# ScalarE's squares of the second token block's first half, moved between two groups of the first block's hand-over

## The chip, the core and the metric

The kernel runs on one core of a Trainium2 chip. The metric is the device time of one execution in microseconds (us), median of three runs.

## What is computed

Two transformer blocks over one sequence of 256 tokens with 1024 features, each with two layers, all in fp32:

```python
# first block, per layer
h = modulate(x, norm_g[l, 0], sh1, sc1)          # rms_norm(x) * g * (1 + scale) + shift
x = x + 0.5 * g1 * swiglu(h, w_ffn1_gu[l], w_ffn1_down[l])
h = modulate(x, norm_g[l, 1], sh2, sc2)
x = x + g2 * (three kinds of attention(h @ w_in[l]) @ w_out[l])
h = modulate(x, norm_g[l, 2], sh3, sc3)
x = x + 0.5 * g3 * swiglu(h, w_ffn2_gu[l], w_ffn2_down[l])
# second block, per layer
h = modulate_2(rmsnorm(x, norm1[l]), sh1, sc1)
x = x + g1 * (retention and pooling branches(h @ w_in[l]) @ w_out[l])
h2 = modulate_2(rmsnorm(x, norm2[l]), sh2, sc2)
x = x + g2 * ((silu(gate) * up) @ w_ffn_out[l])
```

rms_norm divides each token's row by the root of the mean of its squares plus eps. This root needs the squares of all 1024 features of a token.

## The kernel before

The 256 tokens are two token blocks t = 0 and 1 of 128 partitions each (`x[:, t, :]`). The work is ten phases (six in the first block, four in the second), each a list of products of the split activations with streamed weights. An fp32 product is made of three matmuls: `products` (L1911 to L1913) multiplies the high part of the activations with the high and the low part of the weights, and the low part with the high. Weights come by DMA from the SP queue into `weights_raw`. ScalarE rounds a unit of 128x1024 to its high part (`hi_static`, L750), VectorE subtracts to get the low part (`lo_static`, L1221), and TensorE may start a unit when the semaphore `lo_done` has counted it. The order of instructions on every engine is written out by hand; each engine works through its own queue in that order.

Between two phases lies a **hand-over**. There are nine (phase k = 2 to 10 begins with one), and the kernel's end has code of its own. In a hand-over these things happen:

- VectorE (`boundary`) multiplies the four accumulators, two token blocks by two halves of 512 columns, by the gate (L1366) and adds three of them to x (L1372). The add of block 1, first half, is GpSimd's (L732), which then counts `x_late`.
- ScalarE (`norm_stage`) takes the squares of x with their row sums (`squares`, L770; the first half also adds eps, L772), the square root (`root`, L776), waits for VectorE's reciprocal (`x_stats`, L1312), and scales x into `xn` (`scale_x`, L782). For block 1 VectorE scales the first 512 columns in two pieces (`x_scale1`, L1318, semaphore `xn1a_ready`), and ScalarE the last 512 (`xn1b_ready`).
- TensorE turns `xn` (transposes, `x_turn`, L2027) in pairs of 128 columns. With t and the pair that makes eight **groups**: groups 0 to 3 are block 0, groups 4 to 7 block 1.
- Each group is scaled and shifted by the modulation (`x_scaled`: groups 2, 3, 4 and 6 on ScalarE, L791; 0, 1, 5 and 7 on VectorE, L1327), rounded by ScalarE (`x_hi`, L798), and its low part is taken by VectorE (`x_low`, L1336, semaphore `hlo_done`).
- TensorE (`first_strip`) multiplies group by group. In block 0 each group u also uses a new weight unit. The group's first chunk ends with the transposes of block 1's first two pairs only in group 3:

```python
                    if t == 0:
                        pe.wait_ge(S("lo_done"), n + u + 1)
                    pe.wait_ge(S("hlo_done"), tr[0] + g + 1)
                    for c in range(2):
                        if k > 1 and t == 0 and u == 3 and c == 1:
                            x_turn(1, (0, 1), k)
```

Three of the four weight units have their low halves before the hand-over or at its start. The fourth's stands in VectorE's queue right behind the low parts of groups 2 and 3:

```python
                    x_low(2)
                    x_low(3)
                    lo_static(end + PREFETCH - 1, SLOT)
                x_stats(k + 1, 1)
                x_scale1(k + 1)
```

`then` puts a wait behind an instruction: the next one of the same engine starts only when the step has been counted. `squares` uses it after the squares and after the eps.

Of the kernel before, what the change touches and what calls it, by code (L numbers as in the profile page):

```python
# [238 lines left out]
def need(eng, sem, value):  # L239

    if not isinstance(value, int) or value > 0:
        eng.wait_ge(sem, value)


def build(nc, A, out):
    with ExitStack() as ctx:
# [5 lines left out]
        def S(name):  # L252
            if name not in sems:
                sems[name] = ctx.enter_context(nc.semaphore(name))
            return sems[name]
# [170 lines left out]
        def x_group(g, i):  # L426

            t, j = divmod(X_FIRST[g] if i == 0 else g, 4)
            return hf[:, (i + g) % 4, :].rearrange("p (k n) -> p k n", k=2), (slice(2 * j, 2 * j + 2), slice(P * t, P * (t + 1)))

        def x_chunk(g, i, k, first):

            b, c0 = X_AT_FIRST[X_FIRST[g]] if first else X_AT[g]
            return hf[:, (i + g) % 4, P * k:P * (k + 1)], bank[b][:, c0 + P * k:c0 + P * (k + 1)]

        def x_is_scaled(eng, k, g):

            on_act = X_BY_ACT_FIRST if k == 1 else X_BY_ACT
            by = [i for i in range(X_GROUPS) if (i in on_act) == (g in on_act)]
            eng.wait_ge(S("scaled_by_act" if g in on_act else "scaled_by_dve"), len(by) * (k - 1) + by.index(g) + 1)  # L440
# [295 lines left out]
        def _(act):  # L736
            seq = [0]

            def then(ins):

                seq[0] += 1
                ins.then_inc(S("act_step"), 1)
                act.wait_ge(S("act_step"), seq[0])
# [16 lines left out]
            def squares(k, t, h):  # L760

                if k == 1:
                    act.wait_ge(S("x_loaded"), 16)
                elif (t, h) == (1, 0):
                    act.wait_ge(S("x_late"), k - 1)
                else:
                    act.wait_ge(S("x_done"), 3 * (k - 2) + (1, 2, 0, 3)[2 * t + h])
                c = slice(512 * h, 512 * (h + 1))
                at = stat[:, 2 * t + h:2 * t + h + 1]
                then(nc.scalar.activation(xn[:, t, c], x[:, t, c], ACT.Square, scale=D ** -0.5, accum_out=at))  # L770
                if h == 0:
                    then(nc.scalar.activation(at, at, ACT.Identity, bias=stat[:, S_EPS:S_EPS + 1]))  # L772

            def root(k, t):

                nc.scalar.activation(stat[:, 4 + t:5 + t], stat[:, 2 * t + 1:2 * t + 2], ACT.Sqrt, bias=stat[:, 2 * t:2 * t + 1])\  # L776
                    .then_inc(S("rms_ready"), 1)
                act.wait_ge(S("rstd_ready"), 2 * (k - 1) + t + 1)

            def scale_x(t, c0, c1, sem):  # L780

                nc.scalar.activation(xn[:, t, c0:c1], x[:, t, c0:c1], ACT.Copy, scale=stat[:, 6 + t:7 + t]).then_inc(S(sem), 1)  # L782

            def x_scaled(a, g, first=False):

                act.wait_ge(S("tr_ready"), turned[0] + (4 + X_FIRST[g] // 4 * 4 if first else X_TURNED[g]))
                need(act, S("hlo_done"), tr[0] + g - 3)
                for k in range(2):
                    c = 2 * ((X_FIRST[g] if first else g) % 4) + k
                    to, src = x_chunk(g, tr[0], k, first)  # L790
                    ins = nc.scalar.activation(to, src, ACT.Identity, scale=sclA[:, c:c + 1], bias=modc[:, 8 * a["mod"] + c:8 * a["mod"] + c + 1])  # L791
                ins.then_inc(S("scaled_by_act"), 1)

            def x_hi(g):

                src, at = x_group(g, tr[0])
                x_is_scaled(act, o_n[0], g)
                nc.scalar.activation(hhi[:, at[0], at[1]], src, ACT.Copy).then_inc(S("hhi_done"), 1)  # L798
# [5 lines left out]
            def norm_stage(k, after):  # L804

                squares(k, 0, 0)
                squares(k, 0, 1)
                root(k, 0)
                for c0, c1 in ((0, 256), (256, 512), (512, 1024)):
                    scale_x(0, c0, c1, "xn0_ready")  # L810
                if after is not None:
                    split_block0(after)
                squares(k, 1, 0)
                squares(k, 1, 1)
                root(k, 1)
                scale_x(1, 512, 1024, "xn1b_ready")
                if after is not None:
                    split_block1(after)

            def split_block0(after):  # L820

                act.wait_ge(S("scale_ready"), o_n[0])
                x_hi(0)
                x_scaled(after[2], 2)
                x_hi(1)
                x_hi(2)
                x_scaled(after[2], 3)
                x_hi(3)

            def split_block1(after):  # L830

                x_scaled(after[2], 4)
                x_hi(4)
                x_hi(5)
                x_scaled(after[2], 6)
                x_hi(6)
                x_hi(7)
                x_split_done()
# [43 lines left out]
            def first_phase(a):  # L882
# [19 lines left out]
                x_hi(7)  # L902
                x_split_done()
            norm_stage(1, None)

            for kind, n0, a in phases:
                o_n[0] += 1
                if o_n[0] > 1:
                    norm_stage(o_n[0], (kind, n0, a))
                else:  # L910
                    first_phase(a)
# [44 lines left out]
                elif kind == "mid1":  # L956
# [110 lines left out]
                    for h in range(12):  # L1067
                        k = 12 * m + h
# [1496 lines left out]
```

## Time and profile before

| | |
|---|---|
| runs | 1797.13, 1795.12, 1795.99 us; median 1795.99 us |
| the profiled execution's own time | 1796.07 us |
| its span | 1794.2 us |
| granted TensorE clock, mean | 0.997 |
| TensorE matmul busy | 1756.8 us, 98% of the span |
| VectorE busy | 1334.3 us, 74% |
| ScalarE busy | 925.9 us, 52% |
| GpSimd busy | 183.3 us, 10% |

The span runs from the first to the last recorded work; 1.87 us of the execution's own time lie around it. In the trace PE is TensorE (PEld its weight loads), ACT is ScalarE, DVE is VectorE, POOL is GpSimd. Matmuls are pipelined, so that one of 0.39 us starts 0.23 us after the one before it.

### The profile page before, as it was taken

To read this page: it belongs to the slowest core of one execution; us is meant where nothing else is said; L and a number is where in the kernel's file an instruction comes from. 1 tells how busy PE (TensorE), PEld (TensorE's weight loads), DVE (VectorE), ACT (ScalarE), POOL (GpSimd) and SP (SyncE) were. 2 spreads that over 40 slices of the span, in tenths; PEclk is the share of its full clock that TensorE was granted. 3 is DMA by queue.
4 is the path that set the end of the run, shared out by engine and by line. 5 is a ranking of instruction groups with operands and counts; after the bars stand their busy time and mean duration, and the time that the engine had idled before them with its cause. 6 is when DMAs were issued, how large, how long until landed. Compare 5 with 4: busy or idle time off the path is not lost.

```text
span 1794.2 us, 23576 instructions
## 1 busy us (share of the span) xinstructions
PE 1756.8 (98%) x8820; PEld 1449.3 (81%) x8820; DVE 1334.3 (74%) x1977; ACT 925.9 (52%) x1509; POOL 183.3 (10%) x382
## 2 busy tenths in 40 slices
PE   6999999999999999999999999999999999999998
PEld 3778888788878888887888788888888788878886
DVE  6988977778788777768787866478787775677455
ACT  4444577744364345767444644456334644464434
POOL 3111012111111111021110000001110000010000
PEclk9999999999999999999999999999999999999999
DMA  9999832699859885517898664559897484566561
GB/s 328 362 345 368 298 129 75 235 337 336 308 205 353 316 322 204 161 65 270 307 354 291 205 206 156 186 170 329 312 328 262 153 295 156 178 214 237 192 210 72
DMA packets 241874, 441.03 MB, mean 246 GB/s; under 512 B 15248, under 2 KB 157408, under 8 KB 241632
## 3 DMA queue, kind: packets, MB, share of 16 engines
q1 hardware_dynamic: 207760, 315.98, 51.8%
q0 software_dynamic: 33296, 120.12, 17.4%
q10 hardware_dynamic: 704, 3.42, 0.5%
q8 instruction: 70, 1.15, 0.3%
q14 instruction: 44, 0.36, 0.1%
HBM read 438.38 MB, written 1.09 MB: 245 GB/s over the span
## 4 chain that ended last, share of the span: by engine, by line
PE 89%; DVE 5%; ACT 3%; DMA 2%; issue 1%; SPq 0%; DVEq 0%; ACTq 0%
PE bank L1911 27%; PE bank L1913 27%; PE bank L1912 27%; PE bank L2087 2%; DVE weights_lo L1221 1%; DMA weights_raw<-in_w_mod_first 1%; DMA weights_raw<-in_w_ffn_gu 1%; DVE x L1372 1%; DVE arena L1366 1%; PE bank L2277 1%; PE bank L2305 1%; ACT arena L791 0%; ACT hT_hi L798 0%; PE bank L2027 0%; PE bank L2276 0%
## 5 line engine op out<-in xcount | busy, mean ns | idle before, releaser
L1221 DVE TENSOR_TENSOR weights_lo<-weights_raw,weights_hi 128x1024 fp32r<-128x1024 f32 (+2 forms) x584 | 673.1, 1200 | 130.7 <-ACT weights_hi L750 129.6
L1911 PE MATMUL bank<-weights_hi,hT_hi 128*128 128x512 f32 (+2 forms) x1696 | 670.2, 395 | 8.7 <-DVE hT_lo L1336 8.7
L1913 PE MATMUL bank<-weights_hi,hT_lo 128*128 128x512 f32 (+2 forms) x1696 | 658.4, 388 | 0.0
L1912 PE MATMUL bank<-weights_lo,hT_hi 128*128 128x512 f32 (+2 forms) x1696 | 657.2, 388 | 0.0
L750 ACT ACTIVATE weights_hi<-weights_raw 128x1024 fp32r<-128x1024 f32 (+2 forms) x584 | 569.0, 1038 | 103.6 <-PE bank L1913 33.0
L1911 PEld LDWEIGHTS bank<-weights_hi,hT_hi 128*128 128x128 f32 x1696 | 318.6, 188 | 75.6 <-DVE hT_lo L1336 6.7
L1913 PEld LDWEIGHTS bank<-weights_hi,hT_lo 128*128 128x128 f32 x1696 | 318.3, 188 | 65.4
L1912 PEld LDWEIGHTS bank<-weights_lo,hT_hi 128*128 128x128 f32 x1696 | 318.9, 188 | 59.5
L1234 DVE CUSTOM_DVE_ANT_0 arena<-arena,mod_acc,vectors 128x1024 f32<-128x1024 f32 x216 | 264.3, 1279 | 0.0
L926 ACT ACTIVATE actT_hi<-bank 128x512 fp32r<-128x512 f32 x66 | 39.6, 599 | 433.2 <-PE bank L2087 433.2
L1911 PE MATMUL bank<-weights_hi,actT_hi 128*128 128x512 f32 (+1 forms) x616 | 240.1, 390 | 1.9 <-DVE weights_lo L1221 1.4
L1913 PE MATMUL bank<-weights_hi,actT_lo 128*128 128x512 f32 (+1 forms) x616 | 237.9, 386 | 0.0
L1912 PE MATMUL bank<-weights_lo,actT_hi 128*128 128x512 f32 (+1 forms) x616 | 237.8, 386 | 0.0
L1515 DVE TENSOR_TENSOR actT_lo<-bank,actT_hi 128x512 fp32r<-128x512 f32 x66 | 45.6, 690 | 133.2 <-ACT actT_hi L926 133.2
L1911 PEld LDWEIGHTS bank<-weights_hi,actT_hi 128*128 128x128 f32 x616 | 115.6, 188 | 27.9 <-DVE actT_lo L1515 2.8
L1913 PEld LDWEIGHTS bank<-weights_hi,actT_lo 128*128 128x128 f32 x616 | 115.6, 188 | 23.3
L1912 PEld LDWEIGHTS bank<-weights_lo,actT_hi 128*128 128x128 f32 x616 | 115.7, 188 | 22.3
L477 POOL DMA_DIRECT2D arena<-in_w_mod x128 | 67.9, 532 | 362.3 <-DVE mod_cols L1234 359.1
L732 POOL TENSOR_TENSOR x<-x,arena 128x512 f32<-128x512 f32 x10 | 13.2, 1324 | 703.7 <-DVE arena L1366 703.7
L921 ACT ACTIVATE arena<-bank 128x256 f32<-128x256 f32 x132 | 43.6, 383 | 70.3 <-PE bank L1913 70.3
L477 POOL DMA_DIRECT2D arena<-in_w_ada x88 | 46.8, 534 | 258.4 <-DVE mod_cols L1234 251.8
L1510 DVE TENSOR_TENSOR arena<-arena,bank 128x256 f32<-128x256 f32 x132 | 49.2, 414 | 18.9 <-ACT arena L921 18.9
(282 smaller groups left out, 1179.0 us busy)
## 6 DMA issues: line engine op xcount, KB each, us to landing
weights_raw<-in_w_ffn_gu SPq DMA_DIRECT2D x176, 512.0 KB, 5.7
arena<-in_w_mod POOLq DMA_DIRECT2D x128, 512.0 KB, 6.9
weights_raw<-in_w_in SPq DMA_DIRECT2D x104, 512.0 KB, 4.7
weights_raw<-in_w_ffn_down SPq DMA_DIRECT2D x88, 512.0 KB, 5.2
arena<-in_w_ada POOLq DMA_DIRECT2D x88, 512.0 KB, 6.8
weights_raw<-in_w_ffn_in SPq DMA_DIRECT2D x88, 512.0 KB, 5.4
weights_raw<-in_w_ffn_out SPq DMA_DIRECT2D x44, 512.0 KB, 4.5
weights_raw<-in_w_out SPq DMA_DIRECT2D x32, 512.0 KB, 4.2
```

The lines of the kernel that those rows point to most:

```text
L477: eng.dma_start(mod_tile(m), mod_rows(m)).then_inc(S(mod_sem(m)), 16)
L750: nc.scalar.activation(whi[:, n % PARTS, 0:width], raw[:, slot, 0:width], ACT.Copy).then_inc(S("hi_done"), credit(n))
L921: nc.scalar.activation(sg_t[:, t, :], bank[gu_banks(j)[t]][:, 0:256], ACT.Silu).then_inc(S("silu_done"), 1)
L926: nc.scalar.activation(ahi[:, j % 2].rearrange("p k n -> p (k n)"), bank[ATB][:, :], ACT.Copy)\
L1221: V.tensor_tensor(wlo[:, n % PARTS, 0:width], raw[:, n % RING, 0:width], whi[:, n % PARTS, 0:width].bitcast(F32), ALU.subtract).then_inc(S ...
L1234: V.tensor_tensor_reduce(modw[m % MOD_RING], modw[m % MOD_RING], cond_row, 1.0, vec[:, m:m + 1], ALU.mult, ALU.add, modc[:, m:m + 1])\
L1510: ins = V.tensor_tensor(act_t[:, t, :], sg_t[:, t, :], bank[gu_banks(j)[t]][:, 256:512], ALU.mult)
L1515: V.tensor_tensor(alo[:, j % 2].rearrange("p k n -> p (k n)"), bank[ATB][:, :], ahi[:, j % 2].rearrange("p k n -> p (k n)").bitcast(F32), ...
L1911: T.matmul(o, sh, wh, start=start, stop=False)
L1912: T.matmul(o, sh, wl, start=False, stop=False)
L1913: return T.matmul(o, sl, wh, start=False, stop=stop)
L2087: ins = T.transpose(bank[ATB][:, 256 * k + P * t:256 * k + P * (t + 1)], act_t[:, t, P * k:P * (k + 1)], ident)
```

## The change

In each of the nine hand-overs ScalarE's squares of block 1, first half (`squares(k, 1, 0)`: square with row sum, then eps) are issued behind the rounding of group 2 and ahead of the scaling of group 3. They stood behind the rounding of group 3. Phase 1, which has no such split (`after is None`), keeps its order. Nothing is added or left out.

```diff
                 if after is not None:
-                    split_block0(after)
-                squares(k, 1, 0)
+                    split_block0(k, after)
+                if after is None:
+                    squares(k, 1, 0)
                 squares(k, 1, 1)
                 root(k, 1)
                 scale_x(1, 512, 1024, "xn1b_ready")
...
-            def split_block0(after):
+            def split_block0(k, after):
 
                 act.wait_ge(S("scale_ready"), o_n[0])
                 x_hi(0)
                 x_scaled(after[2], 2)
                 x_hi(1)
                 x_hi(2)
+                squares(k, 1, 0)
                 x_scaled(after[2], 3)
                 x_hi(3)
```

ScalarE's queue in the first hand-over, before. `hT_hi` is the rounded group, `arena<-bank4` the scaling of groups 2 and 3, `arena,stat<-x` the squares with row sum, `stat<-stat` first the eps, then the root:

```order
L791 ACTIVATE arena<-bank4,mod_cols,scale_cols 128x128 [waits hlo_done,tr_ready]
L791 ACTIVATE arena<-bank4,mod_cols,scale_cols 128x128
L798 ACTIVATE hT_hi<-arena 128x2x128 [waits scaled_by_dve]
L798 ACTIVATE hT_hi<-arena 128x2x128 [waits scaled_by_act]
L791 ACTIVATE arena<-bank4,mod_cols,scale_cols 128x128 [waits hlo_done,tr_ready]
L791 ACTIVATE arena<-bank4,mod_cols,scale_cols 128x128
L798 ACTIVATE hT_hi<-arena 128x2x128 [waits scaled_by_act]
L770 ACTIVATE arena,stat<-x 128x512 [waits x_late]
L772 ACTIVATE stat<-stat 128x1 [waits act_step]
L770 ACTIVATE arena,stat<-x 128x512 [waits x_done,act_step]
L776 ACTIVATE stat<-stat 128x1 [waits act_step]
L782 ACTIVATE arena<-x,stat 128x512 [waits rstd_ready]
```

The same place in the changed kernel:

```order
L791 ACTIVATE arena<-bank4,mod_cols,scale_cols 128x128 [waits hlo_done,tr_ready]
L791 ACTIVATE arena<-bank4,mod_cols,scale_cols 128x128
L798 ACTIVATE hT_hi<-arena 128x2x128 [waits scaled_by_dve]
L798 ACTIVATE hT_hi<-arena 128x2x128 [waits scaled_by_act]
L770 ACTIVATE arena,stat<-x 128x512 [waits x_late]
L772 ACTIVATE stat<-stat 128x1 [waits act_step]
L791 ACTIVATE arena<-bank4,mod_cols,scale_cols 128x128 [waits hlo_done,tr_ready,act_step]
L791 ACTIVATE arena<-bank4,mod_cols,scale_cols 128x128
L798 ACTIVATE hT_hi<-arena 128x2x128 [waits scaled_by_act]
L770 ACTIVATE arena,stat<-x 128x512 [waits x_done]
L776 ACTIVATE stat<-stat 128x1 [waits act_step]
L782 ACTIVATE arena<-x,stat 128x512 [waits rstd_ready]
```

The pair L770, L772 has moved ahead of group 3's three instructions; the wait on `act_step` behind the eps now stands on the scaling of group 3, no longer on the second squares.

VectorE's queue in the same hand-over is not reordered. It stands so in both kernels (line numbers of before): the low parts of groups 2 and 3, the fourth unit's low half, the reciprocal of block 1, and its first columns scaled:

```order
L1372 TENSOR_TENSOR x<-x,arena 128x512 [waits x_gated]
L1336 TENSOR_TENSOR hT_lo<-arena,hT_hi 128x2x128 [waits hhi_done,scaled_by_act] x2
L1221 TENSOR_TENSOR weights_lo<-weights_raw,weights_hi 128x1024 [waits hi_done]
L1312 RECIPROCAL stat<-stat 128x1 [waits rms_ready]
L1318 TENSOR_SCALAR arena<-x,stat 128x256 [waits rstd_ready]
```

What the second of the two low parts waits for (`hhi_done`) is the rounding of group 3 that the change sets later.

## Rows read from the trace of the kernel before

**Rows 1.** The page, chain of waits that ended last, by engine.

```profile
PE 89%; DVE 5%; ACT 3%; DMA 2%; issue 1%; SPq 0%; DVEq 0%; ACTq 0%
```

**Rows 2.** TensorE's waits: us in total, times, longest.

```profile
PE bank L1911 <- DVE hT_lo L1336: 8.7, 19, 2.5
```

**Rows 3.** Timeline of TensorE, seventh hand-over: start, us, instruction, idle before it.

```profile
1211.60 0.47 PE L1911 MATMUL bank<-weights_hi,hT_hi 128*128 128x512 f32 x1 [0.18 <-DVE hT_lo L1336]
...
1215.86 0.39 PE L1911 MATMUL bank<-weights_hi,hT_hi 128*128 128x512 f32 x1
...
1216.54 0.60 PE L2027 MATMUL bank<-con,arena 128*128 128x128 f32 x4
...
1216.90 0.48 PE L1911 MATMUL bank<-weights_hi,hT_hi 128*128 128x512 f32 x1
...
1218.80 0.50 PE L1911 MATMUL bank<-weights_hi,hT_hi 128*128 128x512 f32 x1 [0.52 <-DVE hT_lo L1336]
...
1219.13 0.39 PE L1912 MATMUL bank<-weights_lo,hT_hi 128*128 128x512 f32 x1
```

**Rows 4.** Timeline of ScalarE, seventh hand-over.

```profile
1211.91 0.72 ACT L798 ACTIVATE hT_hi<-arena 128x256 fp32r<-128x256 f32 x2
1212.52 0.80 ACT L791 ACTIVATE arena<-bank,mod_cols,scale_cols 128x128 f32<-128x128 f32 x2
1213.36 0.42 ACT L798 ACTIVATE hT_hi<-arena 128x256 fp32r<-128x256 f32 x1
1213.68 0.62 ACT L770 ACTIVATE arena<-x 128x512 f32<-128x512 f32 x1
1214.20 0.19 ACT L770 ACTIVATION_READ_ACCUMULATOR arena<-x 128x1 f32 x1
1214.42 0.29 ACT L772 ACTIVATE stat<-stat 128x1 f32<-128x1 f32 x1
1214.75 0.63 ACT L770 ACTIVATE arena<-x 128x512 f32<-128x512 f32 x1
...
1215.51 0.29 ACT L776 ACTIVATE stat<-stat 128x1 f32<-128x1 f32 x1
```

**Rows 5.** Timeline of VectorE, seventh hand-over.

```profile
1211.03 0.42 DVE L1336 TENSOR_TENSOR hT_lo<-arena,hT_hi 128x256 fp32r<-128x256 f32 x1 [0.30 <-ACT hT_hi L798]
...
1213.37 0.93 DVE L1336 TENSOR_TENSOR hT_lo<-arena,hT_hi 128x256 fp32r<-128x256 f32 x2
1214.22 1.22 DVE L1221 TENSOR_TENSOR weights_lo<-weights_raw,weights_hi 128x1024 fp32r<-128x1024 f32 x1
1215.83 0.16 DVE L1312 RECIPROCAL stat<-stat 128x1 f32<-128x1 f32 x1 [0.39 <-ACT stat L776]
1216.03 0.62 DVE L1318 TENSOR_SCALAR arena<-x,stat 128x256 f32<-128x256 f32 x2
...
1218.32 0.42 DVE L1336 TENSOR_TENSOR hT_lo<-arena,hT_hi 128x256 fp32r<-128x256 f32 x1 [0.41 <-ACT hT_hi L798]
```

**Rows 6.** Timeline of GpSimd, seventh hand-over.

```profile
1209.29 1.27 POOL L732 TENSOR_TENSOR x<-x,arena 128x512 f32<-128x512 f32 x1 [174.78 <-DVE arena L1366]
```

**Rows 7.** Timeline of VectorE, fourth and fifth hand-over: the fourth unit's low half.

```profile
718.44 1.21 DVE L1221 TENSOR_TENSOR weights_lo<-weights_raw,weights_hi 128x1024 fp32r<-128x1024 f32 x1
...
827.67 1.22 DVE L1221 TENSOR_TENSOR weights_lo<-weights_raw,weights_hi 128x1024 fp32r<-128x1024 f32 x1
```

**Rows 8.** Timeline of TensorE, fourth and fifth hand-over: first matmul of group 3.

```profile
720.18 0.39 PE L1911 MATMUL bank<-weights_hi,hT_hi 128*128 128x512 f32 x1
...
829.24 0.39 PE L1911 MATMUL bank<-weights_hi,hT_hi 128*128 128x512 f32 x1
```

**Rows 9.** Stretches early in phase 1: busy time (count) of each engine, then PEclk.

```profile
22.00:24.00 2.00, 1.78 (x52) 0.95 (x53) 1.21 (x4) 0.76 (x3) 0.00 (x0) 0.53 1.01 406
24.00:26.00 2.00, 2.00 (x16) 1.37 (x14) 1.90 (x7) 1.54 (x2) 0.00 (x0) 0.61 1.07 422
...
34.00:36.00 2.00, 0.71 (x6) 0.50 (x5) 1.96 (x6) 1.06 (x4) 0.00 (x0) 1.00 0.87 309
```

## The prediction

> **What bounds the kernel now.** I read the chain of waits first: 89% of it is TensorE's own work [rows 1]. So a change can pay, or cost, only where TensorE stands still. TensorE's list of waits is next: its largest wait beyond the very start is for the low part of the activations (L1336), 8.7 us in 19 times, the longest 2.5 us [rows 2]. That longest one is in phase 1. The other 18 are two in each of the nine hand-overs: 0.18 us before group 0 and about half a microsecond before group 4 (0.18 and 0.52 us in the seventh [rows 3]). The timelines of the nine hand-overs are alike to a tenth of a microsecond, so I work in the seventh and scale up.
>
> The order of events there is what a reader should see. TensorE starts group 3 at 1215.86, turns block 1's first pairs at 1216.54, goes on at 1216.90, and stands before group 4, which starts at 1218.80 [rows 3]. ScalarE has **no gap** where the change works: rounding of groups 1 and 2 (1211.91, two), scaling of 3 at 1212.52, rounding of 3 at 1213.36, squares at 1213.68, eps at 1214.42, second squares at 1214.75, root at 1215.51 [rows 4]. None of these rows carries an idle time. VectorE takes the low parts of groups 2 and 3 from 1213.37 to 1214.30, then the low half of the fourth weight unit from 1214.22 to 1215.44, then waits 0.39 us for ScalarE's root and takes the reciprocal at 1215.83 [rows 5].
>
> **The moved block.** It is two instructions, squares with row sum and eps. From its start to the start of the next squares it takes 1214.75 - 1213.68 = 1.07 us of ScalarE [rows 4]. The Trainium skill would have it shorter: its page "ScalarE: Activation LUTs", section "What ACT_TABLE_LOAD costs", gives 186 ns + 0.833 ns a column for an ACTIVATE with immediates, 93 ns more for a pointer operand, and 93 ns of overlap between neighbours, which I make an estimate of 613 + 280 - 93 = 800 ns. The rows show why that is not the block here: the read of the row sum (0.19 us at 1214.20) and the wait for it lie between the two [rows 4]. By the page's 0.80 the sum below would be 9 x (0.80 + 0.06 + 0.10) - 3.74 = 4.90 us, by the row it is 7.33; I take the row.
>
> **What becomes earlier: nothing that counts.** Squares and eps move to about 1212.5, where the scaling of group 3 stands now, but the second squares cannot start earlier: the engine has the same instructions ahead of them, with no gap to fill. The wait on the eps moves from the second squares to the scaling of group 3, and is as long there (eps ends at 1214.71, next start 1214.75 [rows 4]). So root 1 stays at 1215.51. Its own wait for GpSimd's addition costs nothing: that ends at 1209.29 + 1.27 = 1210.56, two microseconds before the squares' new place [rows 4, 6]. No DMA is issued by the block, and no table load stands at either place.
>
> **What becomes later.** Scaling and rounding of group 3, by 1.07 us. The rounding ends at 1213.36 + 0.42 = 1213.78; the low part of group 3 starts at 1214.30 - 0.42 = 1213.88, 0.10 us behind it [rows 4, 5]. So VectorE already follows ScalarE here, and goes back with it in full: the fourth unit's low half starts at 1214.22 + 1.07 = 1215.29 and ends at 1216.51. **TensorE needs this unit for group 3** (its wait on lo_done), which it now starts at 1215.86. Before, the low half was ready at 1215.44, 0.42 us early; now it is late. The slack is the start of group 3 less the end of the low half. Over the nine hand-overs it is 0.50, 0.37, 0.42, 0.53, 0.35, 0.38, 0.42, 0.38 and 0.39 us, together 3.74; the largest is the fourth (720.18 - 719.65), the smallest the fifth (829.24 - 828.89) [rows 7, 8].
>
> Behind the end of a VectorE instruction TensorE needs a moment. Group 4 starts 0.06 us after the low part's end (1218.32 + 0.42 = 1218.74 to 1218.80), group 0 needs 0.15 (1211.45 to 1211.60) [rows 3, 5]. Group 3's wait, with matmuls running right up to it, is nearer to the first in kind (only the instruction just before differs), so 0.06; 0.15 is kept as the high end. A stopped stream also starts slowly: after the wait the second matmul comes 0.33 us behind the first (1218.80, 1219.13), where three in flow take 1216.54 - 1215.86 = 0.68, 0.23 each [rows 3]. That is 0.10 us more; the low end is none.
>
> In the seventh: 1.07 - 0.42 + 0.06 + 0.10 = **0.81 us**. In all nine: 9 x (1.07 + 0.06 + 0.10) - 3.74 = **7.33 us**.
>
> **Is it given back?** After group 3's first chunk come the transposes of block 1, and all up to group 4 hangs on them: 1218.80 - 1216.54 = 2.26 us [rows 3]. They would be at 1217.35. What they need is VectorE's scaled columns. The reciprocal now stands behind the late low half: at about 1216.43 instead of 1215.83, 0.60 us later, so the two pieces end at 1216.65 + 0.60 = 1217.25 [rows 5], just in time. ScalarE's part of the scaling follows the same reciprocal and is back by 1217.35, ahead of the scaling of group 4. So the wait before group 4 keeps its half microsecond, and behind it TensorE works without a stop up to the next hand-over, so that there is no gap in which it could catch up. At most the transposes lose the few hundredths that some hand-overs now wait for the second piece. The last hand-over, at the kernel's end, is untouched.
>
> **The sum.** 1796.07 (the profiled execution) + 7.33 = 1803.40; that execution is 0.08 us above the median, so 1803.3. The bounds: without the slow start and the 0.06, 9 x 1.07 - 3.74 = 5.89, which is 1801.9; with 0.15 for the semaphore, 8.14, which is 1804.1. Runs of this kernel lie about 1 us to either side of their median.
>
> **Rivals.** *No change:* the late low half is covered after all, because TensorE does not stand at group 3 when it comes. For it: the shift is only 0.65 us beyond the slack. Against it: TensorE's timeline has group 3 directly behind group 2 in all nine, with no gap. It decides if the shift is under 0.42 us. Time: 1796.0. *Faster:* the squares fill a gap of ScalarE, root and reciprocal come up to 1.07 us earlier, and the wait before group 4 goes. That wait is (8.7 - 2.5 - 9 x 0.18) = 4.6 us in all [rows 2, 3], so 1791.4. It would need ScalarE to stand idle between the rounding of group 2 and the scaling of group 3 for longer than the slack it spends; the rows show no idle there at all, and the transposes could not start before group 3's first chunk ends anyway [rows 3, 4]. *The clock falls:* TensorE would stand still for 0.7 us more, and soon after for 0.5. Early in phase 1 the granted clock was 0.53 and 0.61 in two stretches of 2 us, between the levels of 1.2 and 2.4 GHz, after a stretch of small matmuls with gaps; in 34 to 36 us TensorE stood still for most of the time and the clock stayed at 1.00 [rows 9]. Such a dip would cost 2 x 0.47 + 2 x 0.39 = 1.7 us, nine of them 15.5 us: 1818.8. The Trainium skill ("TensorE: Matmul & The Clock Gate", "What's actually happening") has the throttled state as the default that activity lifts. By that rule more idle time speaks for this rival; the stretch at full clock beside the wait of 2.5 us [rows 2, 9] speaks against it.
>
> **Chances.** Forecast 0.87; no change 0.07; faster 0.03; clock 0.03. A difference of 0.2%, 3.6 us, is about what a measurement of this kernel can tell from none. The forecast and the clock case are slower by more than that: 0.90. No change is 0.07, faster 0.03. The range is the forecast's own, since it alone holds 8 in 10: from 1801.9 and 1804.1, widened by the spread of runs of 1.1 us at both ends: 1800.7 to 1805.3.
>
> **What would show it.** In the changed profile: a new wait of TensorE ahead of group 3 (line 1911, now 1913) for the weights' low half (line 1221, now 1223), nine times, 0.6 to 0.8 us each. The squares directly behind the rounding of group 2; VectorE idle about 1 us before the second low part and none before the reciprocal; the wait before group 4 still about 0.5 us; the root at the same distance from group 0. Wrong would be: group 3 directly behind group 2; the root earlier; the wait before group 4 gone or doubled; granted clock below 1 in a hand-over.

## The result and the profile after

| | before | changed |
|---|---|---|
| median of six runs each | 1796.22 us (1794.81 to 1797.15) | 1802.54 us (1802.15 to 1804.65) |
| ratio, with its 95% interval | | 1.0036 [1.0026, 1.0047] |
| the profiled execution's own time | 1796.07 us | 1802.21 us |
| its span | 1794.2 us | 1800.4 us |
| VectorE, ScalarE busy | 1334.3, 925.9 us | 1334.0, 925.5 us |
| granted TensorE clock, mean | 0.997 | 0.997 |

The change makes the kernel slower by 0.36%, 6.3 us. A second set of six runs (below) gave 1802.93 against 1795.76, 7.2 us. The forecast was 1803.3 us, with a range of 1800.7 to 1805.3.

TensorE's waits in the changed kernel (us in total, times, longest) are to be held against [rows 2]. The lines of the kernel have moved by two:

```profile
PE bank L1913 <- DVE hT_lo L1338: 8.9, 19, 2.5
PE bank L1913 <- DVE weights_lo L1223: 6.5, 10, 1.3
```

The kernel before has this row in place of the second:

```profile
PE bank L1911 <- DVE weights_lo L1221: 1.4, 1, 1.4
```

The first row is what it was, 8.7 before and 8.9 now. In the second, TensorE now waits for a low half of weights ten times. One of these, the longest, is in phase 1 and was there before. The other nine are new, one in each hand-over, ahead of group 3, of 0.47, 0.61, 0.59, 0.56, 0.59, 0.58, 0.60, 0.56 and 0.59 us, together 5.15.

TensorE in the seventh hand-over (start, us, instruction, idle before it), to be held against [rows 3]. Group 0 started at 1215.29:

```profile
1219.26 0.39 PE L1915 MATMUL bank<-weights_hi,hT_lo 128*128 128x512 f32 x1
1220.25 0.50 PE L1913 MATMUL bank<-weights_hi,hT_hi 128*128 128x512 f32 x1 [0.60 <-DVE weights_lo L1223]
1220.58 0.39 PE L1914 MATMUL bank<-weights_lo,hT_hi 128*128 128x512 f32 x1
...
1221.04 0.60 PE L2029 MATMUL bank<-con,arena 128*128 128x128 f32 x4
...
1223.30 0.50 PE L1913 MATMUL bank<-weights_hi,hT_hi 128*128 128x512 f32 x1 [0.53 <-DVE hT_lo L1338]
```

Group 3 starts at 1220.25 after a wait of 0.60 us for the weights' low half; the next matmul comes 0.33 us behind it. From the transposes at 1221.04 on everything keeps its old distances: group 4 comes 2.26 us later, after the same half microsecond of waiting.

ScalarE at the same place, to be held against [rows 4]:

```profile
1215.58 0.72 ACT L798 ACTIVATE hT_hi<-arena 128x256 fp32r<-128x256 f32 x2
1216.20 0.63 ACT L770 ACTIVATE arena<-x 128x512 f32<-128x512 f32 x1
1216.72 0.20 ACT L770 ACTIVATION_READ_ACCUMULATOR arena<-x 128x1 f32 x1
1216.95 0.29 ACT L772 ACTIVATE stat<-stat 128x1 f32<-128x1 f32 x1
1217.28 0.81 ACT L791 ACTIVATE arena<-bank,mod_cols,scale_cols 128x128 f32<-128x128 f32 x2
1218.12 0.42 ACT L798 ACTIVATE hT_hi<-arena 128x256 fp32r<-128x256 f32 x1
1218.44 0.62 ACT L770 ACTIVATE arena<-x 128x512 f32<-128x512 f32 x1
...
1219.18 0.29 ACT L776 ACTIVATE stat<-stat 128x1 f32<-128x1 f32 x1
1220.30 0.73 ACT L782 ACTIVATE arena<-x,stat 128x512 f32<-128x512 f32 x1 [0.83 <-DVE stat L1314]
```

The squares and the eps stand between the rounding of group 2 and the scaling of group 3, and take 1217.28 - 1216.20 = 1.08 us. The root is at 1219.18. Behind it ScalarE waits 0.83 us for the reciprocal; in the kernel before it waits 0.23 us there. VectorE, against [rows 5]:

```profile
1218.64 0.43 DVE L1338 TENSOR_TENSOR hT_lo<-arena,hT_hi 128x256 fp32r<-128x256 f32 x1 [1.17 <-ACT hT_hi L798]
1218.98 1.22 DVE L1223 TENSOR_TENSOR weights_lo<-weights_raw,weights_hi 128x1024 fp32r<-128x1024 f32 x1
1220.11 0.15 DVE L1314 RECIPROCAL stat<-stat 128x1 f32<-128x1 f32 x1
1220.30 0.67 DVE L1320 TENSOR_SCALAR arena<-x,stat 128x256 f32<-128x256 f32 x2
```

It waits 1.17 us for the rounding of group 3, takes its low part, then the fourth unit's low half, and comes to the reciprocal with no wait of its own. Counted from the start of group 0, in us (the forecast worked out from the prediction's numbers):

| seventh hand-over | before | forecast | changed |
|---|---|---|---|
| rounding of group 3 ends | 2.18 | 3.25 | 3.25 |
| fourth unit's low half starts | 2.62 | 3.69 | 3.69 |
| root of block 1 | 3.91 | 3.91 | 3.89 |
| reciprocal of block 1 | 4.23 | 4.83 | 4.82 |
| group 3 starts | 4.26 | 4.97 | 4.96 |
| transposes of block 1 | 4.94 | 5.75 | 5.75 |
| group 4 starts | 7.20 | 8.01 | 8.01 |

### The profile page after: what moved, and what is told of

It is laid out like the page before. It is cut to its first block, busy times and chain, and to the rows that moved or that the text cites. A ratio compares the mean times of both kernels' runs of the same rounds, so it can differ in the third digit from the quotient of the medians.

```text
span 1800.4 us, 23567 instructions
## 1 busy us (share of the span) xinstructions
PE 1759.2 (98%) x8820; PEld 1448.7 (80%) x8820; DVE 1334.0 (74%) x1977; ACT 925.5 (51%) x1509; POOL 184.9 (10%) x382
## 3 DMA queue, kind: packets, MB, share of 16 engines
HBM read 438.38 MB, written 1.09 MB: 244 GB/s over the span
## 4 chain that ended last, share of the span: by engine, by line
PE 87%; DVE 5%; ACT 4%; DMA 2%; issue 1%; SPq 0%; DVEq 0%; ACTq 0%
PE bank L1913 26%; PE bank L1915 26%; PE bank L1914 26%; DVE weights_lo L1223 2%; PE bank L2089 2%; ACT arena L791 1%; PE bank L2029 1%; DMA weights_raw<-in_w_mod_first 1%; ACT hT_hi L798 1%; DMA weights_raw<-in_w_ffn_down 1%; DVE x L1374 1%; DVE arena L1368 1%; ACT arena L770 1%; PE bank L2279 1%; PE bank L2307 1%
```

## The experiments

**The low half ahead of group 3's low part, in the changed kernel and in the one before.** If the fourth unit's low half is what TensorE waits for, it has only to stand ahead of the late group in VectorE's queue. The same swap in the kernel before is the control.

```diff
                     x_low(2)
-                    x_low(3)
                     lo_static(end + PREFETCH - 1, SLOT)
+                    x_low(3)
```

> The changed kernel, with the fourth unit's low half put ahead of the low part of group 3 in VectorE's queue. Theory (TensorE waits for that low half, which only stands behind the late group 3): it is ready at about 1.07 us less of a delay, the low part of group 3 ends about 0.4 us before TensorE comes to group 3, so the nine waits ahead of group 3 go, group 0 to group 4 takes 7.20 us as in the kernel before (8.02 in the changed one), and the time is that of before, 1796.2, within 1 us. Rival (the moved squares cost by themselves, through ScalarE or through the late group 3): the wait stays under another name and the time stays near 1802.5.

> The kernel before, with the same swap on VectorE and ScalarE's queue untouched. Theory (both were ready 0.35 us or more early): no change, 1796.2 within 1 us, no wait ahead of group 3. Rival (the swap is a gain or a loss of its own, so that the run above says nothing of the change): over 2 us off 1796.2.

Measured: the changed kernel with the swap 1796.74 us against 1795.93, ratio 1.0004 [0.9995, 1.0013]; the kernel before with it 1795.90, ratio 1.0005 [0.9996, 1.0014]. Neither differs from the kernel before by more than the runs can tell. VectorE in the changed kernel with the swap, seventh hand-over:

```profile
1214.89 1.22 DVE L1223 TENSOR_TENSOR weights_lo<-weights_raw,weights_hi 128x1024 fp32r<-128x1024 f32 x1
1216.15 0.43 DVE L1338 TENSOR_TENSOR hT_lo<-arena,hT_hi 128x256 fp32r<-128x256 f32 x1
1217.02 0.16 DVE L1314 RECIPROCAL stat<-stat 128x1 f32<-128x1 f32 x1 [0.44 <-ACT stat L776]
```

and TensorE (group 0 at 1212.77):

```profile
1217.03 0.39 PE L1913 MATMUL bank<-weights_hi,hT_hi 128*128 128x512 f32 x1
...
1219.97 0.50 PE L1913 MATMUL bank<-weights_hi,hT_hi 128*128 128x512 f32 x1 [0.52 <-DVE hT_lo L1338]
```

The low half ends at 1216.11, 0.92 us ahead of group 3's start at 1217.03. The low part of group 3, as late as in the changed kernel, still ends 0.45 us ahead. Group 4 starts 7.20 us after group 0, as before the change. Over all nine hand-overs the stretches from group 0 to group 4 are 64.80 us in this run and 64.84 in the control, against 64.85 in the kernel before and 72.22 in the changed one. The moved squares and the late group 3 themselves cost nothing: the loss is the one item queued behind them.

**Without the squares.** The rival "faster" rests on the root: would an earlier root remove the wait ahead of group 4?

```diff
-                squares(k, 1, 0)
+                if after is None:
+                    squares(k, 1, 0)
+                else:
+                    act.wait_ge(S("x_late"), k - 1)
                 squares(k, 1, 1)
```

> The kernel before without the squares of block 1, first half, in the nine hand-overs (left out: that half's part in the root; its wait for GpSimd's addition stays). ScalarE's root comes 1.07 us earlier. Theory (the transposes of block 1 are held by their place in TensorE's queue, behind group 3's first chunk, not by the root): the wait of half a microsecond ahead of group 4 stays and the time is 1795.8 to 1796.2, at most 0.05 us a hand-over better. Rival (the root sets the wait ahead of group 4): the wait goes, 1791.6.

Measured: 1795.23 us against 1795.93, ratio 0.9997 [0.9988, 1.0006]. That is 0.6 us below the range that was expected, but no difference that the runs can tell, and nowhere near the rival's 1791.6. Group 0 of the seventh hand-over started at 1211.64. ScalarE (root, scaling of x, scaling of group 4) and TensorE (transposes, group 4):

```profile
1214.46 0.29 ACT L776 ACTIVATE stat<-stat 128x1 f32<-128x1 f32 x1
1215.58 0.73 ACT L782 ACTIVATE arena<-x,stat 128x512 f32<-128x512 f32 x1 [0.83 <-DVE stat L1315]
1216.96 0.81 ACT L791 ACTIVATE arena<-bank,mod_cols,scale_cols 128x128 f32<-128x128 f32 x2 [0.65 <-PE bank L2030]
```

```profile
1216.54 0.60 PE L2030 MATMUL bank<-con,arena 128*128 128x128 f32 x4
...
1218.80 0.50 PE L1914 MATMUL bank<-weights_hi,hT_hi 128*128 128x512 f32 x1 [0.54 <-DVE hT_lo L1339]
```

The root now starts 2.82 us after group 0, 1.09 earlier than the 3.91 of before, and ScalarE stands idle behind it twice, for 0.83 and 0.65 us (0.23 and 0.21 before). The transposes come 4.90 us after group 0 (4.94 before), and group 4 still waits 0.54 us. Groups 0 to 4 take 64.78 us over the nine, 0.07 less than before. The root has slack, so no move of the squares alone could have gained anything.

**Less of the moved work.** If the cost is what the moved block exceeds the slack by, a shorter block must cost less. The eps stays in its old place, so the block is shorter by the pitch of one instruction (the argument True leaves the eps out of `squares`).

```diff
                 if after is None:
                     squares(k, 1, 0)
+                else:
+                    then(nc.scalar.activation(stat[:, 2:3], stat[:, 2:3], ACT.Identity, bias=stat[:, S_EPS:S_EPS + 1]))
...
-                squares(k, 1, 0)
+                squares(k, 1, 0, True)
                 x_scaled(after[2], 3)
```

> The changed kernel with the eps (L772) left in its old place, behind the rounding of group 3; only the square with its row sum stands ahead of the scaling of group 3. Theory (the cost is what the moved block exceeds the slack of the fourth unit's low half by): the block is 0.74 us instead of 1.07, so TensorE's waits ahead of group 3 shrink by 0.33 us each to 0.15 to 0.3 us, group 0 to group 4 takes 7.68 us in the seventh hand-over, and the time is 9 x (0.74 + 0.16) - 3.74 = 4.4 us over before, 1800.4. Rival (a broken stream costs a fixed amount, however late the unit is): as the changed kernel, 1802.5.

Measured: 1802.04 us (1799.55 to 1806.5) against 1796.27, ratio 1.0034 [1.0021, 1.0046]. By the median alone the rival would have it, but these six runs spread over 7 us. The hand-overs decide. TensorE in the seventh, groups 0, 3 and 4:

```profile
1216.97 0.47 PE L1915 MATMUL bank<-weights_hi,hT_hi 128*128 128x512 f32 x1 [0.18 <-DVE hT_lo L1340]
...
1221.62 0.50 PE L1915 MATMUL bank<-weights_hi,hT_hi 128*128 128x512 f32 x1 [0.28 <-DVE weights_lo L1225]
...
1224.68 0.50 PE L1915 MATMUL bank<-weights_hi,hT_hi 128*128 128x512 f32 x1 [0.52 <-DVE hT_lo L1340]
```

The wait ahead of group 3 is 0.28 us, where the changed kernel has 0.60, and group 4 comes 7.71 us after group 0, against 7.68 expected and 8.01 in the changed kernel. Over the nine, groups 0 to 4 take 4.6 us more than before (4.4 expected). The profiled execution took 1803.02 us; the rest of its time over the kernel before lies ahead of the first hand-over, which it reaches at 231.36 us, where the kernel before does so at 228.99. So the cost does follow the size of the block, as the hand-overs show; six runs that spread over 7 us cannot show it.

**A block shorter than the slack.** One short instruction of eps' kind stands in the squares' new place; the squares are left out so that the root can't interfere.

```diff
                 x_hi(2)
+                then(nc.scalar.activation(table_col[:, :], ones_col, ACT.Identity, bias=stat[:, S_EPS:S_EPS + 1]))
                 x_scaled(after[2], 3)
```

> The kernel of the run without the squares of block 1, first half (left out again), with one instruction of eps' length and a wait on it (on a scratch column, about 0.33 us) between the rounding of group 2 and the scaling of group 3. Theory (a block shorter than the slack of 0.35 to 0.53 us costs nothing): no wait ahead of group 3 above 0.05 us, group 0 to group 4 7.2 us, 1795.2 to 1796.2. Rival (every delay of group 3 is paid from its first nanosecond): 9 x 0.33 = 3.0 us, 1798.9.

Measured: 1796.77 us against 1796.27, ratio 1.0003 [0.9994, 1.0012]: 0.6 us above the range that was expected, but not the 3.0 us of the rival. VectorE (low part of group 3, low half) and TensorE (group 3 and group 4; group 0 at 1212.20), seventh hand-over:

```profile
1214.80 0.42 DVE L1340 TENSOR_TENSOR hT_lo<-arena,hT_hi 128x256 fp32r<-128x256 f32 x1 [0.41 <-ACT hT_hi L798]
1215.14 1.22 DVE L1225 TENSOR_TENSOR weights_lo<-weights_raw,weights_hi 128x1024 fp32r<-128x1024 f32 x1
```

```profile
1216.42 0.49 PE L1915 MATMUL bank<-weights_hi,hT_hi 128*128 128x512 f32 x1
1216.75 0.40 PE L1916 MATMUL bank<-weights_lo,hT_hi 128*128 128x512 f32 x1
...
1219.47 0.50 PE L1915 MATMUL bank<-weights_hi,hT_hi 128*128 128x512 f32 x1 [0.53 <-DVE hT_lo L1340]
```

No wait is listed ahead of group 3. But the low half ends at 1216.36, group 3 starts 0.06 us behind it, and its second matmul follows after 0.33 us, not 0.23. Groups 0 to 4 take 7.27 us. The nine hand-overs differ. In seven the low half ends 0.05 to 0.08 us ahead of group 3, and the second matmul comes after 0.31 to 0.34 us. In the first and the fourth it ends 0.22 and 0.21 us ahead, the second matmul comes after 0.23 us, and nothing is lost. Over the nine groups 0 to 4 take 0.76 us more than before, so the expectation of 7.2 was missed by a little: a unit that comes just in time costs a tenth of a microsecond though no wait shows.

**Statistics ahead of group 3.** If TensorE's order of transposes is what keeps the root from paying, both must move together. The root of block 1 goes ahead of group 3 on ScalarE, what depends on it goes ahead on VectorE, and on TensorE the transposes of block 1's first two pairs go ahead of group 3 and so fill the time in which it is not ready. (`sqrt_only` is `root` without its wait for the reciprocal, which now stands behind the rounding of group 3. The cut is against the changed kernel, and its definition is left out.)

```diff
                 if after is None:
                     squares(k, 1, 0)
-                squares(k, 1, 1)
-                root(k, 1)
+                    squares(k, 1, 1)
+                    root(k, 1)
...
                 squares(k, 1, 0)
+                squares(k, 1, 1)
+                sqrt_only(k, 1)
                 x_scaled(after[2], 3)
                 x_hi(3)
+                act.wait_ge(S("rstd_ready"), 2 * (k - 1) + 2)
...
                     x_low(2)
-                    x_low(3)
                     lo_static(end + PREFETCH - 1, SLOT)
                 x_stats(k + 1, 1)
                 x_scale1(k + 1)
                 if after is not None:
+                    x_low(3)
...
+                    if k > 1 and t == 0 and u == 3:
+                        x_turn(1, (0, 1), k)
                     if t == 0:
                         pe.wait_ge(S("lo_done"), n + u + 1)
                     pe.wait_ge(S("hlo_done"), tr[0] + g + 1)
                     for c in range(2):
-                        if k > 1 and t == 0 and u == 3 and c == 1:
-                            x_turn(1, (0, 1), k)
```

> Both halves' squares of block 1 and the root ahead of the scaling of group 3 on ScalarE; on VectorE the fourth unit's low half, the reciprocal and the two scaled pieces ahead of the low part of group 3; on TensorE the transposes of block 1's first two pairs ahead of group 3's first chunk, not behind it. Theory: group 3 is ready about 0.6 us late, but 0.36 us of that are filled by the transposes, and group 4's parts are ready as soon as TensorE comes to them: group 0 to group 4 takes about 6.7 us instead of 7.20, 1791.7 in all. Rival (the wait only moves ahead of group 3, whose rounding now stands behind 2.1 us of statistics): 7.2 to 7.6 us and 1796 to 1800.

Measured: 1792.47 us against 1795.93, ratio 0.9983 [0.9975, 0.9992]. It beats both kernels, if by 0.8 us less than expected. TensorE in the seventh hand-over (group 0, transposes, group 3, transposes, group 4):

```profile
1209.77 0.47 PE L1920 MATMUL bank<-weights_hi,hT_hi 128*128 128x512 f32 x1 [0.20 <-DVE hT_lo L1345]
...
1213.97 0.60 PE L2036 MATMUL bank<-con,arena 128*128 128x128 f32 x4
1214.63 0.47 PE L1920 MATMUL bank<-weights_hi,hT_hi 128*128 128x512 f32 x1
...
1216.08 0.60 PE L2036 MATMUL bank<-con,arena 128*128 128x128 f32 x4
1216.44 0.47 PE L1920 MATMUL bank<-weights_hi,hT_hi 128*128 128x512 f32 x1
1216.75 0.39 PE L1921 MATMUL bank<-weights_lo,hT_hi 128*128 128x512 f32 x1
```

Group 4 starts 6.67 us after group 0, and it does not wait any more (6.7 expected; 7.20 before). Over the nine hand-overs groups 0 to 4 take 60.24 us, 4.6 less than before. Yet from group 0 of the first hand-over to the end the profile is only 3.2 us shorter (table below), and the median 3.5. Most of the difference is given back in the two attention phases of the first block. Two rows of TensorE's list of waits:

```profile
PE bank L2138 <- DVE arena L1586: 1.2, 2, 0.6
PE bank L2036 <- ACT arena L786: 0.7, 1, 0.7
```

The first is 0.59 us in each of the two phases, where it was 0.19 and 0.14 before (L2129): 0.9 us given back. The second is the wait for ScalarE's scaled x at the end of the first of these phases. It scatters: 0.67 us here, 0.20 when this kernel was run again (below), 0.09 in the kernel before. In the other phases the stretch up to the next hand-over is 0.01 to 0.07 us longer each.

The trace shows where the first wait comes from. TensorE starts group 4 of the first hand-over 0.48 us earlier than before (6.80 us after group 0 against 7.28), but the last step of VectorE that it waits for has hardly moved. That step before, with group 0 at 228.99, and then in this run, with group 0 at 228.84:

```profile
247.30 0.28 DVE L1577 TENSOR_SCALAR arena<-arena,stat 128x128 f32<-128x128 f32 x1
```

```profile
247.11 0.28 DVE L1586 TENSOR_SCALAR arena<-arena,stat 128x128 f32<-128x128 f32 x1
```

It ends 18.59 us after group 0 before and 18.55 here. Ahead of it on VectorE stand the low halves of four weight units, which follow their rounding on ScalarE, and ScalarE's last rounding in that hand-over ends 8.46 us after group 0 before and 8.43 here. This is read from the trace; no run isolates it. Nor does this run, which moves work on three engines at once, show what each of the moves is worth by itself.

**Both once more, on one chip.** The changed kernel's median was 6.3 us above the kernel before, though its hand-overs were 7.4 us longer.

> The changed kernel once more, on the chip of the next run. The nine hand-overs' distances from group 0 to group 4 were 7.37 us longer in all in its profile, its median only 6.3 us longer over six runs, and the stretch ahead of the first hand-over, whose instructions are the same, was 1.0 us shorter. Theory (that stretch scatters from run to run, the hand-overs do not): from group 0 of the first hand-over to the end it is again 7.2 us longer than in the kernel before, within 0.3, and the median difference comes out at 7 us, within 1.5. Rival (about 1 us of the loss is given back ahead of the first hand-over): that stretch is again about 1 us shorter, and the median difference stays at 6.3 or below.

> The kernel with block 1's statistics ahead of group 3 once more. Theory: from group 0 of the first hand-over to the end 3.2 us shorter than in the kernel before, within 0.5, and a median 3.2 us shorter, within 1.5: nine times 0.53 us, less what two waits in the attention phases give back (about 0.5 us each) and a scattered wait. Rival (it gains nothing beyond scatter): within 1 us of the kernel before.

Measured: the changed kernel 1802.93 us against 1795.76, ratio 1.0044 [1.0031, 1.0057]; with the statistics ahead 1792.36, ratio 0.9981 [0.9972, 0.9989]. The profiled executions, split at group 0 of the first hand-over:

| kernel | ahead of it | from there to the end |
|---|---|---|
| before | 228.99 | 1567.08 |
| changed | 227.97 | 1574.24 |
| changed, once more | 228.90 | 1574.44 |
| changed, low half first | 229.83 | 1567.39 |
| before, low half first | 228.25 | 1567.33 |
| without the squares | 229.10 | 1566.91 |
| square alone moved | 231.36 | 1571.66 |
| short block | 229.20 | 1567.74 |
| statistics ahead of group 3 | 228.84 | 1563.90 |
| the same once more | 228.41 | 1563.60 |

The changed kernel loses 7.2 and 7.4 us behind that point, as the theory had it (7.2 within 0.3), and ahead of it is once 1.0 shorter and once as long as before. Nothing is given back there; that stretch scatters. With the statistics ahead of group 3 the kernel is 3.2 and 3.5 us shorter behind that point, and 3.4 in the second median.

## Why the prediction was right

- **The price of the block** was read as 1.07 us; it takes 1.08 in its new place. The estimate of 0.80 us from the Trainium skill ("ScalarE: Activation LUTs", "What ACT_TABLE_LOAD costs") would have given 4.9 us in all. The nine hand-overs lost 7.37, so the row was the better price here. Most of the difference lies ahead of the eps: it starts 0.75 us after the square (1216.95 - 1216.20), behind the read of the row sum and the wait on it.
- **Nothing that counts becomes earlier:** the root stands at 3.89 us after group 0, where it was at 3.91. Taking the squares out altogether (a root 1.09 us earlier) gained no measurable time, so even this could not have paid.
- **The whole shift goes through VectorE to the fourth unit:** its low half starts 1.07 us later. The run with the two steps of VectorE swapped shows that this is the only path: the same late group 3, and no loss (64.80 us over the nine, against 64.85).
- **The slack** of 3.74 us over the nine hand-overs, the 0.06 us to TensorE and the slow start of 0.10 us gave 0.81 us in the seventh, and 0.81 us were measured (8.01 - 7.20). The sum was 7.33 us; group 0 to group 4 took 72.22 us in all, before 64.85, so 7.37. The 0.06 us is 0.05 to 0.06 in all nine, and the second matmul comes 0.33 to 0.34 us behind the first. The bounds that set the slow start or the semaphore otherwise (5.89 and 8.14) were not needed. The prediction called the nine hand-overs alike to a tenth of a microsecond, which was a little too even: group 3 stood 4.20 to 4.38 us after group 0. The sum was safe from this because it took each slack by itself. In the changed kernel group 3 stands at 4.96 to 4.98 in all nine: VectorE now sets its start.
- **The listed wait** was misjudged: 0.6 to 0.8 us were named as the sign, 0.47 to 0.61 are listed. Group 3 starts 0.70 us later, as it should, but a listed wait begins only at the recorded end of the matmul before it (1219.26 + 0.39 = 1219.65), 0.16 us behind the point where a matmul in flow would have started. The sum does not use it.
- **Nothing is given back:** the transposes came at 5.75, as forecast, just behind VectorE's pieces; the wait ahead of group 4 stayed at 0.53 us. One reason given for it was wrong: TensorE does not work "without a stop up to the next hand-over". In the attention phases the kernel before has waits of 0.09 to 0.31 us, so there was room to catch up. It was not used: from group 4 to the next group 0, or to the end, the nine stretches take 1500.38 us before and 1500.21 in the changed kernel.
- **The rivals.** No change would have needed cover for the late half, and there was none. Faster would have needed a root that counts, or a gap in ScalarE. The clock stayed at full level in spite of 5.15 us more of waiting. The stretch of the changed kernel that holds all nine hand-overs (busy time and count of each engine, then PEclk, which is 1.00):

```profile
228.00:1620.00 1392.00, 1378.21 (x6661) 1143.26 (x6662) 1040.79 (x1575) 744.40 (x1245) 137.64 (x296) 1.00 0.68 239
```

- **The time** was 0.8 us below the forecast at first and 0.4 us below it when measured again, both within what the runs scatter.

## What to carry to other kernels

Moving work earlier on an engine without a gap delays whatever it is moved past, so follow each of those items to the engine that waits for it, and then everything queued behind the waiting instruction there; the loss here was in a weight unit that has nothing to do with the squares. The cost is the shift less the slack of the first item that TensorE needs, plus what restarting its stream takes (0.06 and 0.10 us a place here), so measure that slack at each place before the edit. The earlier root alone was worth nothing; a gain came in the run that moved TensorE's transposes and VectorE's steps with it. How much of it is due to each was not measured.

## What had not been expected

- The stretch ahead of the first hand-over takes from 227.97 to 231.36 us in the ten profiles of this study, with the same instructions in it. Behind it the kernel before and the two with the low half first lie within 0.3 us of each other (1567.08 to 1567.39). It is likely that this stretch also makes most of the scatter of the medians; only the profiled executions show it. In the longest, TensorE waits 2.01 us for a weight unit's low half, up to 57.07 us, where the kernel before has no wait, and the granted clock is 0.50 from 56.6 to 60.0 us. Differences of a microsecond or two are better read from a point inside the trace than from the whole time: the first measurement of the changed kernel, 6.3 us, and the second, 7.2 us, belong to the same 7.2 to 7.4 us.
- A stream of matmuls that is fed just in time has no listed wait, but its second matmul comes 0.31 to 0.34 us behind the first, not 0.23 (the short block, above). It cost 0.76 us over nine places, of which seven paid.
- With the statistics ahead of group 3, 0.9 us of the gain went into two later waits of the attention phases, where TensorE had become early for VectorE.
